# Two-block transformer kernel on one core: attention groups placed between the projection units of the last phase, a weight ring of four units

## What is computed

```python
h = rms_norm(x, g_pre)
a_qkv, bq, bk, bv, mq, ga, gb, gm, mg = split(h @ w_in)
# branch a: rope on q and k; three dilated windows; softmax weights from their log-denominators
oa = sum_g wts[g] * dilated_window_attention(aq[g], ak[g], av[g], window[g], dil[g])
# branch b: grouped-query attention, normalised q and k, axial rope, no mask
ob = softmax(qb_ @ kb_.T * 64**-0.5) @ vb_
# branch m: attention to 256 memory tokens
om = softmax(mq @ km.T * 128**-0.5) @ vm
ya, yb, ym = ((o * silu(g)) @ w for o, g, w in ((oa, ga, w_br_a), (ob, gb, w_br_b), (om, gm, w_br_m)))
gates = sigmoid(mg + b_merge)
x = x + rms_norm((gates[0]*ya + gates[1]*yb + gates[2]*ym) @ w_out, g_post)
```

## Time and profile before

| what | value |
|---|---|
| median of three runs | 2755.66 us |
| the profiled execution: time | 2755.64 us |
| the profiled execution: span of its instructions | 2753.8 us |
| PE busy | 2623.4 us (95%) |
| DVE busy | 1814.1 us (66%) |
| ACT busy | 1251.1 us (45%) |
| chain that ended last, by engine | PE 84%, DVE 12%, ACT 2% |
| mean granted TensorE clock | 0.983 of full |

### The profile page before, as it was taken

How to read it: one execution, slowest core, us unless ns; L and a number is a source line. 1 busy time by engine, 2 the same in 40 slices (tenths; PEclk the granted TensorE clock), 3 DMA queues, 4 the chain that set the end, 5 groups by cost and what they waited for, 6 DMA issues and landing times.

```text
span 2753.8 us, 49774 instructions
## 1 busy us (share of the span) xinstructions
PE 2623.4 (95%) x21152; PEld 2562.4 (93%) x21152; DVE 1814.1 (66%) x2256; ACT 1251.1 (45%) x1323; POOL 5.2 (0%) x13
## 2 busy tenths in 40 slices
PE   8999899999999999999969999999899999799997
PEld 8999899999998999999959999999799998688897
DVE  6557876586566755765676568556976577566565
ACT  4346554444344544544454345446454355332443
POOL 0000000000000000000000000000000000000000
PEclk9999999999999999999989999999999999999999
DMA  7555045545552555455415544544245544133251
GB/s 286 181 181 180 32 172 198 181 155 186 182 181 93 188 183 183 153 199 183 167 50 184 181 179 150 196 182 153 92 159 182 183 174 178 57 112 138 79 184 45
DMA packets 60204, 435.51 MB, mean 158 GB/s; under 512 B 6720, under 2 KB 6848, under 8 KB 7584
## 3 DMA queue, kind: packets, MB, share of 16 engines
q1 hardware_dynamic: 59184, 429.05, 43.2%
q0 software_dynamic: 880, 4.39, 0.4%
HBM read 432.37 MB, written 1.05 MB: 157 GB/s over the span
## 4 chain that ended last, share of the span: by engine, by line
PE 84%; DVE 12%; ACT 2%; issue 1%; DMA 0%; ACTq 0%; DVEq 0%
PE ps L608 56%; PE ps L635 18%; PE ps L621 4%; DVE w_lo L1365 2%; ACT w_hi L1012 1%; PE ps L868 1%; DVE xg_lo L1410 1%; DVE xg_hi L1407 1%; PE ps L848 1%; PE ps L858 1%; DVE x L1471 1%; DVE scratch L1641 1%; DVE scratch L1797 1%; DVE scratch L1653 1%; DVE scratch L1631 1%
## 5 line engine op out<-in xcount | busy, mean ns | idle before, releaser
L1365 DVE TENSOR_TENSOR w_lo<-raw,w_hi 128x2048 fp32r<-128x2048 f32 x407 | 932.1, 2291 | 504.7 <-ACT w_hi L1012 503.9
L608 PE MATMUL ps<-xg_hi,w_hi 128*128 128x256 f32 x4240 | 1212.6, 286 | 29.4 <-DVE xg_lo L1410 24.9
L608 PE MATMUL ps<-xg_hi,w_lo 128*128 128x256 f32 x4240 | 1201.2, 283 | 0.0
L608 PE MATMUL ps<-xg_lo,w_hi 128*128 128x256 f32 x4240 | 1201.1, 283 | 0.0
L1012 ACT CAST w_hi<-raw 128x2048 fp32r<-128x2048 f32 x407 | 772.4, 1898 | 491.4 <-PE ps L635 247.9
L608 PEld LDWEIGHTS ps<-xg_hi,w_hi 128*128 128x128 f32 x4240 | 808.2, 191 | 38.6 <-issue 23.6
L608 PEld LDWEIGHTS ps<-xg_hi,w_lo 128*128 128x128 f32 x4240 | 808.4, 191 | 2.9 <-issue 2.4
L608 PEld LDWEIGHTS ps<-xg_lo,w_hi 128*128 128x128 f32 x4240 | 808.2, 191 | 0.0
L635 PE MATMUL ps<-mo_hi,w_hi 128*128 128x256 f32 x1568 | 445.1, 284 | 3.7 <-DVE xg_hi L1407 3.7
L635 PE MATMUL ps<-mo_hi,w_lo 128*128 128x256 f32 x1568 | 443.9, 283 | 0.0
L635 PE MATMUL ps<-mo_lo,w_hi 128*128 128x256 f32 x1568 | 443.8, 283 | 0.0
(11 more groups left out here) (262 smaller groups left out, 2298.9 us busy)
## 6 DMA issues: line engine op xcount, KB each, us to landing
raw<-weights_dram SPq DMA_DIRECT2D x407, 1024.0 KB, 4.8
x<-x_t_dram SPq DMA_DIRECT2D x1, 1024.0 KB, 7.5
scratch<-p_t_dram POOLq DMA_DIRECT2D x4, 256.0 KB, 3.1
scratch<-mem_t_dram POOLq DMA_DIRECT2D x1, 1024.0 KB, 6.5
scratch<-c_second_dram POOLq DMA_DIRECT2D x1, 1024.0 KB, 5.2
out_dram<-x SPq DMA_DIRECT2D x2, 512.0 KB, 2.6
common<-c_common_dram POOLq DMA_DIRECT2D x1, 640.0 KB, 9.0
scratch<-c_levels_dram POOLq DMA_DIRECT2D x1, 448.0 KB, 7.7
```

The costliest lines, as they stand in the source:

```text
L608: last = nc.tensor.matmul(bank(e)[:, half * T:(half + 1) * T], l, r, start=(k == 0 and j == 0 and half == 0), stop=(k == KC - 1 and j == 2 ...
L1365: V.tensor_tensor(w_lo[:, m % SPLIT, :], raw[:, m % RAW, :], w_hi[:, m % SPLIT, :].bitcast(F32), ALU.subtract).then_inc(weights_split, 1)
```

## The change

- Attention groups are no longer in stages of their own. `group_steps` (one on each engine) gives functions for the single steps of a group. Between two projection units of the next stage stands one group (units 10 to 27) or two (units 28 to 33): the values of the group before, the transposes of this one, the scores of the next one. The stages with their groups are: units 10 to 18 with the six wide groups, units 19 to 27 with the eight narrow groups of the first half, units 28 to 33 with those of the second half.
- The banks are dealt out anew for these 24 units: projections have banks 0 and 1, the rotation bank 2, scores 3 and 4, transposes 5 and 6, values 7. Wide groups have one buffer, narrow groups two.
- The gates and branches go in the order b, m, a. Each half of branch a has q, k and v in a place of its own, so the scratch grows from 15360 to 18176 columns; for that `raw` has 4 slots instead of 6. The loops of the SwiGLU phases run four steps a turn instead of two, twelve units, so that a turn is a multiple of the ring.
- The 1 MB of constants for the last phase is loaded near the start of the program instead of in the last phase.

The diff, cut to its core. First the ring, the loops and PE:

```diff
+BRANCHES = (1, 2, 0)
-RAW = 6
+RAW = 4
+ROUND = 4
...
-            def project(n, e, a, operand_ready=None, by=1, dn=0, de=0):
+            def project(n, e, a, operand_ready=None, by=1, dn=0, de=0, ring=BANKS):
                 pe.wait_ge(weights_split, n + 1 + dn)
-                pe.wait_ge(bank_read, e + 1 + de)
+                pe.wait_ge(bank_read, e + 1 + BANKS - ring + de)
...
-                with pe.Fori(0, (STEPS - 3) // 2) as it:
-                    for s in (2, 3):
+                with pe.Fori(0, (STEPS - 3) // ROUND) as it:
+                    for s in range(2, 2 + ROUND):
...
+            def group_steps(g0, groups, wide):
+                depth = 1 if wide else 2
+                def scores(g):
+                    if g >= len(groups):
+                        return
+                    if g < depth:
+                        pe.wait_ge(att["exp"], g0)
+                    else:
+                        pe.wait_ge(att["exp" if wide else "bias"], g0 + g + 1 - depth)
...
+                    for col, n, q, k in groups[g]["scores"]:
+                        o = group_banks(g, wide, 3)[:, col:col + n]
+                        last = nc.tensor.matmul(o, q, k, start=True, stop=True)
+                    last.then_inc(att["scores"], 1)
+                def turn(g):
+                    if g >= len(groups):
+                        return
+                    pe.wait_ge(att["probs"], g0 + g + 1)
+                    pe.wait_ge(att["pt"], g0 + max(g + 1 - depth, 0))
...
+                def values(g):
+                    if not 0 <= g < len(groups):
+                        return
+                    pe.wait_ge(att["pt"], g0 + g + 1)
+                    pe.wait_ge(att["taken"], g0 + g)
...
-                attention(att_before(i, 0), memory_groups() + branch_b, ATT_2, late=True)
...
+                    scores(0)
+                    for u in range(9):
+                        n, e = n0 + u0 + u, e0 + u0 + u
+                        if u < 6:
+                            project(n, e, XG, ring=2)
+                        else:
+                            project_tokens(n, e, XG, ring=2)
+                        if 0 < u < 7:
+                            rotate(u - 1)
+                        values(u - 1)
+                        turn(u)
+                        scores(u + 1)
...
+                scores(0)
+                scores(1)
+                for u in range(6):
+                    project(n0 + 28 + u, e0 + 28 + u, XG, ring=2)
+                    for g in (2 * u, 2 * u + 1):
+                        values(g - 2)
+                        turn(g)
+                        scores(g + 2)
                 banks_clear(att_before(i, 4))
-                for u in range(28, 34):
-                    project(n0 + u, e0 + u, XG)
+                pe.wait_ge(bank_read, e0 + 34 + 4)
```

ACT:

```diff
                 for half in range(2):
+                    exps(0)
                     for u in range(9):
+                        copies(u)
+                        exps(u + 1)
                         high(n0 + 10 + 9 * half + u + SPLIT)
-                    attention(att_before(i, 2 + half), dilated_groups(), ATT_A)
+                exps(0)
+                exps(1)
...
                 for u in range(6):
                     act.wait_ge(bank_read, e0 + 28 + u + 5)
                     t = SE_GATE[u % 2]
                     nc.scalar.activation(t, t, ACT.Silu).then_inc(m["gate"], 1)
+                    for g in (2 * u, 2 * u + 1):
+                        copies(g)
+                        exps(g + 2)
                     high(n0 + 28 + u + SPLIT)
```

DVE:

```diff
                 for half in range(2):
                     u0 = 10 + 9 * half
+                    logits(0)
+                    if not half:
+                        rope_sines()
+                    probs(0)
+                    for u in range(9):
+                        n, e = n0 + u0 + u, e0 + u0 + u
+                        if u < 6:
+                            scale(n, e, SE_X[u % 2], ring=2)
+                        else:
+                            scale_tokens(n, e, VA[:, :, 256 * (u - 6):256 * (u - 5)], 0, ring=2)
+                        if 0 < u < 7:
+                            dst = (QA if u < 4 else KA)[:, 2 * ((u - 1) % 3):2 * ((u - 1) % 3) + 2]
+                            rope(3 + 6 * half + u - 1, SE_X[(u - 1) % 2], dst)
+                        take(u - 1)
+                        logits(u + 1)
+                        if u == 0 and not half:
+                            rope_rest(0)
+                            rope_rest(1)
+                            rope_rest(2)
+                        low(n + SPLIT)
+                        probs(u + 1)
...
+                logits(0)
+                logits(1)
+                probs(0)
+                probs(1)
                 for u in range(6):
...
+                    scale(n0 + 28 + u, e0 + 28 + u, t, ring=2)
+                    for g in (2 * u, 2 * u + 1):
+                        take(g - 2)
+                        logits(g + 2)
                     dve.wait_ge(m["gate"], u + 1)
...
                     low(n0 + 28 + u + SPLIT)
+                    probs(2 * u + 2)
+                    probs(2 * u + 3)
```

More of the change, by code:

```diff
@@ L910, in banks_clear @@
             def banks_clear(g):
-                for what in ("exp", "pt", "taken"):
+                for what in ("bias", "exp", "pt", "taken"):
                     pe.wait_ge(att[what], g)
@@ L945, in second, with rotate @@
                 pe.wait_ge(bank_read, e0 + 10 + 4)
[L946 to L947 removed]
+                first = memory_and_b()
+                for G in first[2:]:
                     G["ready"] = (m["roped"], 3)
[L949 removed]
                 for half in range(2):
                     u0 = 10 + 9 * half
[L952 to L954 removed]
+                    groups = dilated_groups(0) if half else first
+                    scores, turn, values = group_steps(att_before(i, 2 * half), groups, half == 0)
+                    def rotate(p):
@@ L971, in second @@
-                    pe.wait_ge(m["roped"], 9 + 6 * half)
-                    attention(att_before(i, 2 + half), dilated_groups(), ATT_A, read="bias")
+                    if half:
+                        pe.wait_ge(m["roped"], 9)
+                    scores(0)
[10 more added lines that the diff above has]
+                        scores(u + 1)
@@ L1192, in ml, with group_steps, exps, copies @@
                 gates_out(i, m, n0 + 8, e0 + 8, ML_T, ACT.Sigmoid)
+            def group_steps(g0, groups, wide):
+                depth = 1 if wide else 2
+                def exps(g):
+                    if g >= len(groups):
+                        return
+                    G = groups[g]
+                    t = tiny[:, 32 * (g % 3):32 * (g % 3) + 32]
+                    act.wait_ge(att["bias"], g0 + g + 1)
+                    if wide:
+                        act.wait_ge(att["turned"], g0 + g)
+                    for s in range(G["slots"]):
+                        part = slice(s * G["width"], (s + 1) * G["width"])
+                        p = probabilities(g, wide)[:, part]
+                        src = group_banks(g, wide, 3)[:, part] if wide else p
+                        last = nc.scalar.activation(p, src, ACT.Exp, bias=t[:, 4 + s:5 + s], scale=G["scale"],
+                                                    accum_out=t[:, 8 + s:9 + s])
+                    last.then_inc(att["exp"], 1)
+                def copies(g):
+                    if g >= len(groups):
+                        return
+                    act.wait_ge(att["turned"], g0 + g + 1)
+                    act.wait_ge(att["out"], g0 + max(g + 1 - depth, 0))
+                    nc.scalar.copy(turned_probabilities(g, wide), group_banks(g, wide, 5)).then_inc(att["pt"], 1)
+                return exps, copies
             def attention(g0, groups, bufs, sinks=False, from_psum=False):
@@ L1937, in second @@
[L1937 to L1941 removed]
+                    QA, KA, VA = SE_A[half]
@@ new lines, in second @@
+                    if half:
+                        logits, probs, take = group_steps(att_before(i, 2), dilated_groups(0), False, place_a(0))
+                    else:
+                        logits, probs, take = group_steps(att_before(i, 0), memory_and_b(), True, place)
+                    logits(0)
[6 more added lines that the diff above has]
+                            scale(n, e, SE_X[u % 2], ring=2)
+                        else:
+                            scale_tokens(n, e, VA[:, :, 256 * (u - 6):256 * (u - 5)], 0, ring=2)
[10 more added lines that the diff above has]
+                        probs(u + 1)
```

218 lines of the change are left out of this document (130 added, 88 removed).

## The result

The changed kernel takes 2729.24 us (median of four runs, 2724.58 to 2731.89); the kernel before took 2755.34 beside it. The ratio is 0.9903, 95% interval 0.9891 to 0.9914. The forecast was 2732, its range 2713 to 2747. The profiled execution took 2730.69 us with a span of 2728.9.

A forecast was written before the change was run, and what follows sets the result against it. In the attention stages PE waits for DVE and runs partly at half clock. A bound of 45.2 us, less 19.3 of waits and 2 for the clock, gave a gain of 24: 2755.6 to 2732 us, 8-in-10 range 2713 to 2747.

The forecast's parts named there:

- The stretch and its bound: First attention group to end of unit 33, 260.2 us: PE's work is 215.0 us, so at most 45.2 us gained.
- The ring through DVE and ACT: Logits to logits, DVE and ACT work in series without overlap: 12.1 us a wide step, 10.4 a narrow one.
- The waits: PE waits before transposes: 9.0 us in units 10 to 18, 7.3 in 19 to 27, 3.0 in 28 to 33.
- The gate stage: Units 28 to 33: three steps waiting 0.6 us each, 0.4 for a take, 0.8 at the end; 3.0 us.
- The sum: Whole stretch: upper bound 45.2 us, less 19.3 of waits, less 2 for the clock; gain 24 us.
- The clock: Five waits in the stretch lie near the border; two clock falls taken, 2 us together, ends 0 and 10 us.
- Rivals 2 and 3: Clock falls in the stretch: rival 2, gain only 3 to 14 us, chance 0.17; rival 3, slower than before, chance 0.05.
- The table loads: At the gates ACT alternates silu and exponential; loads cost nothing, or 3.8 us if three are uncovered.
- Ring of four and loops: Outside the stretch: four-step loops neutral within 1 us; four load slots free, with loads landing 7.7 us ahead.
- Rival 1: In the stretch PE never waits, or under 0.3 us a step: gain 40 to 45 us, 2711 to 2716; chance 0.15.

The follow-up runs named there:

- the kernel with high first: The changed kernel with ACT making the high part of the next weight unit before the next group's exponentials, not after: 2714.29 us, ratio 0.9854 to the kernel before.
- the second profile: Profile from running the changed kernel once more, nothing altered, beside other runs on the same chip: 2729.18 us, ratio 0.9913 to the kernel before.
- the kernel with the gate stage apart: The changed kernel with the last attention stage's eight groups in front of the six gate units again, not between them: 2742.38 us, ratio 0.9950.
- the one with longer waits: The changed kernel with one more ACT copy of 1024 columns before the exponentials of each of four branch b groups: 2734.49 us, ratio 0.9934.
- the one with one table: The changed kernel with the exponential in place of silu at the six gate units, leaving one function table for the stretch: 2729.6 us, ratio 0.9916.

## Why the prediction was right, and where it wasn't

- *The stretch and its bound.* Right. 27.7 of the 45.2 us that could be won were won, and the kernel with high first shows that the bound of PE's work, 215.0 us, was real: it needs 218.9, with 2.7 of them waits. The stretch of the changed kernel is 232.5 us, just under the 234 to 238 forecast.
- *The ring through DVE and ACT.* Right in kind and place, and shown by the exchange of two instructions on ACT. Its size was somewhat high: 11.55 to 11.8 us for a wide step, not 12.1, and 10.05 for a narrow one, not 10.4. The terms that were mis-sized are mostly DVE's: an instruction can start before the one in front has ended, so operations that last 0.69 us take 0.60 of the ring each (the rows at 2391.79 to 2392.99), and the four multiplies, put at 1.4, take 1.14. The forecast added up durations where it should have added starts to starts.
- *The waits.* 9.0, 7.3 and 3.0 us were forecast. The wide stage had 0.57, 1.07, 1.77, 1.52 and 1.52: 6.5 us. The narrow one had 3.0: 0.45 at the head, none in the next three steps, then 0.49, 0.49 and 0.23 instead of 1.0 each, and 1.30 instead of 2.0 at the last group. A difference of 0.4 us in the ring halves a wait of 1 us. Timeline of PE in the narrow stage:

```profile
2481.49 0.66 PE L880 MATMUL ps<-common,scratch 128*128 128x128 f32 x4 [0.49 <-DVE scratch L1901]
...
2491.54 0.66 PE L880 MATMUL ps<-common,scratch 128*128 128x128 f32 x4 [0.49 <-DVE scratch L1901]
```

- *The gate stage.* A wait was overlooked. The walk let two values matmuls follow each other in unit 31, but all groups now share one bank for the values, so the second waits for the take of the first's; and that take stood on DVE behind the making of branch b's low part (1.22 us) and a scale. It shows in the timeline of PE, with the end of the stretch, and in that of DVE:

```profile
2560.36 0.66 PE L880 MATMUL ps<-common,scratch 128*128 128x128 f32 x4 [0.31 <-DVE scratch L1901]
2562.97 1.73 PE L891 MATMUL ps<-scratch 128*64 128x128 f32 x8 [1.95 <-DVE scratch L1909]
2564.62 1.12 PE L880 MATMUL ps<-common,scratch 128*128 128x128 f32 x4
...
2573.41 1.06 PE L891 MATMUL ps<-scratch 128*64 128x128 f32 x8 [0.48 <-DVE scratch L1909]
2581.50 0.36 PE L656 MATMUL ps<-mo_hi,w_hi 128*128 128x256 f32 x1 [1.09 <-DVE scratch L1528]
```

```profile
2560.81 1.22 DVE L2113 TENSOR_TENSOR mo_lo<-scratch,mo_hi 128x1024 fp32r<-128x1024 f32 x1
...
2562.55 0.27 DVE L1909 COPY scratch<-ps 64x128 f32<-64x128 f32 x1
```

  The three waits of 0.3, the 1.95, 0.48 and 1.09 are 4.4 us, 1.4 more than forecast. This missing term and the ring's excess are of opposite sign, so the total of the waits, 13.9 us against 19.3, is nearer than its parts deserve.
- *The sum.* The forecast had 215.0 us of PE's work, 19.3 of waits and 2 for the clock, 236.3 in all; measured are 218.6 of busy time and 13.9 of waits, 232.5. Of the 218.6 some 1.5 are the fall of the clock at 2563 us (the second profile, without it, has 217.1), so the work itself was put 2 us too low. The stretch thus gave 27.7 us, 3.7 more than the 24 forecast; 24.9 lie between the two spans, because 2.8 us were lost outside. That the total came within 1 to 2 us (26.1 by the medians) is in part luck.
- *The clock.* Two falls were put at the waits near 2 us. In units 10 to 27 there was none: the clock is 1.00 in both windows. One stands behind the wait of 1.95 us (clock 0.97 in the gate stage), not in each execution; the other, at 2693 us, behind the stretch and behind a wait of 1.77 us that the kernel before has too. Between a wait of 2.09 us with a fall and one of 1.78 without, the forecast saw a border; the runs show none (see the last section). Rivals 2 and 3 are right in that long waits cost clock, as the 20 us at half clock in the kernel with the gate stage apart show. But behind the waits of the interleaved stages the clock fell seldom and for 3.4 us, not for 13.6. That the projection in each step is the reason is an argument; no run took it away alone. The rule of the Trainium skill on the swinging clock (TensorE: Matmul & The Clock Gate, A second HAM failure mode: psum-queue depth-cycling) isn't borne out here: banks go round and PE idles shortly in most steps, and the clock is 1.00 in those windows.
- *The table loads.* Right: nothing.
- *Ring of four and loops.* Right: ratio 0.9998, and in the changed kernel no `high` waits for a load after the start of the program.
- *Rival 1* (PE never waits, 2711 to 2716) did not come about, but its condition, that `high` comes early, gives just its time when it is made true: 2714.

## What to carry to other kernels

When groups of a latency-bound stage are put between units of a throughput-bound one, don't only sum each engine's work: follow one item round all engines in the order of their queues, from start to start, and compare that ring with the work of the busiest engine. If the ring is longer, look for an instruction in it that doesn't belong to it (here the weight copy, which could run as well in the wait for the logits) and put it in the time in which its engine waits. And whatever lost its second buffer needs its reader looked up on the other engine: that reader now ends a wait.

## What was unexpected of the hardware

- A wait of PE doesn't by itself fix whether the clock falls. The same wait of 1.95 us in the gate stage was followed by a fall in two of four profiles (the first of the changed kernel and the one with longer waits, not the second and not the one with one table); waits of 2.01 and 2.45 us passed without one, one of 2.70 us was followed by 3.4 us at half clock. The ten profiles of this case show it more sharply still: near the end, all kernels have the same wait of 1.76 or 1.77 us for a low part made by DVE (`mo_lo`), with the same projection behind it. In five it was followed by a fall of 3.4 us, in five (the kernel before among them) by none. The falls also explain part of the scatter of single executions: of the four runs of the changed kernel the two with a mean clock of 0.988 took 2730.69 and 2731.89 us, those with 0.990 and 0.991 took 2727.80 and 2724.58.
- A load of a function table (1.28 us) is issued as soon as the instruction before it has ended, ahead of the wait of the operation that needs it: below, the load for silu starts at 2534.08 us, and the silu at 2538.21, behind a wait for DVE. So the load cost nothing where ScalarE waited anyway. The Trainium skill (ScalarE: Activation LUTs, What ACT_TABLE_LOAD costs) adds a drain of about 1.4 us to a switch. No drain shows here: in the changed kernel's timeline of ACT the exponential starts right behind the load, 0.01 us later.

```profile
2534.08 1.28 ACT L1415 ACT_TABLE_LOAD   x1
2538.21 0.63 ACT L1415 ACTIVATE scratch<-scratch 128x512 f32<-128x512 f32 x1 [2.85 <-DVE scratch L1528]
...
2539.33 1.28 ACT L1286 ACT_TABLE_LOAD   x1
2540.62 0.72 ACT L1286 ACTIVATE scratch<-scratch,tiny 128x512 f32<-128x512 f32 x1
```
